# Reading turned activations and ready-made vector columns at the opening of a two-block transformer kernel

## The reference

```python
def rmsnorm(x, g):
    xf = x.astype(jnp.float32)
    y = xf * lax.rsqrt(jnp.mean(xf * xf, axis=-1, keepdims=True) + EPS)
    return (y * g.astype(jnp.float32)).astype(x.dtype)

h = rmsnorm(x, pre_mix_g[l])
proj = h @ w_in[l]

def ada_modulation(cond, w, b):
    m = jax.nn.silu(cond) @ w + b
    return jnp.split(m[..., None, :], N_MOD, axis=-1)
```

## Time and profile before

| | |
|---|---|
| Median of 3 runs | 2143.29 us (2139.48 to 2143.92) |
| Profiled execution | 2144.96 us, span 2143.3 us |
| PE busy | 2119.4 us, 99% |
| DVE busy | 1563.8 us, 73% |
| ACT busy | 1092.7 us, 51% |
| POOL busy | 128.7 us, 6% |
| DMA | 487.10 MB, mean 227 GB/s; 332 GB/s in the first of 40 slices |
| Granted TensorE clock | 0.999 |

### The profile page before, as it was taken

One profiled execution on the slowest core, in us unless ns is written; L12 is line 12 of the kernel. 1 busy time (PEld: TensorE's weight loads), 2 busy tenths in 40 slices (PEclk: granted clock), 3 DMA queues, 4 the chain that ended last, 5 costly groups with the idle time before them and its releaser, 6 DMA issues.

```text
span 2143.3 us, 33221 instructions
## 1 busy us (share of the span) xinstructions
PE 2119.4 (99%) x10603; PEld 1764.0 (82%) x10603; DVE 1563.8 (73%) x1943; ACT 1092.7 (51%) x1499; POOL 128.7 (6%) x231
## 2 busy tenths in 40 slices
PE   8999999999999999999999999999999999999998
PEld 7888888888888888888878867888888888888886
DVE  7997889888998888768777654567556656655766
ACT  6545755655444554345587465454434434443444
POOL 3110000100000100100000000010000000000000
PEclk9999999999999999999999999999999999999999
DMA  9887177888888888877756542667667766766763
GB/s 332 293 272 243 40 281 239 279 292 275 280 285 288 276 289 272 293 252 243 238 180 199 184 130 80 196 203 245 202 197 235 217 196 221 231 188 216 221 182 108
DMA packets 279985, 487.10 MB, mean 227 GB/s; under 512 B 26252, under 2 KB 118740, under 8 KB 278560
## 3 DMA queue, kind: packets, MB, share of 16 engines
q1 hardware_dynamic: 249472, 371.42, 53.5%
q0 software_dynamic: 30192, 113.72, 16.5%
q10 hardware_dynamic: 176, 0.08, 0.0%
HBM read 483.00 MB, written 2.11 MB: 226 GB/s over the span
## 4 chain that ended last, share of the span: by engine, by line
PE 95%; ACT 2%; DVE 2%; DMA 1%; issue 1%; POOL 0%; ACTq 0%; DVEq 0%; POOLq 0%
PE G L2020 20%; PE G L2022 20%; PE G L2021 20%; PE G L2035 6%; PE T L2035 6%; PE G L2037 3%; PE T L2037 3%; PE T L2022 3%; PE T L2020 3%; PE T L2021 3%; PE T L2234 1%; PE T L2318 1%; PE T L2468 1%; ACT w_hi L602 1%; PE T L2074 1%; PE G L2450 1%
## 5 line engine op out<-in xcount | busy, mean ns | idle before, releaser
L1144 DVE TENSOR_TENSOR w_lo<-raw,w_hi 128x1024 fp32r<-128x1024 f32 (+1 forms) x704 | 851.8, 1217 | 470.1 <-ACT w_hi L602 466.8
L602 ACT ACTIVATE w_hi<-raw 128x1024 fp32r<-128x1024 f32 (+1 forms) x704 | 741.4, 1055 | 822.9 <-PE G L2022 532.8
L2020 PE MATMUL G<-w_hi,h_both 128*128 128x512 f32 (+1 forms) x1144 | 447.1, 391 | 2.0 <-DVE h_both L1236 1.7
L2022 PE MATMUL G<-w_hi,h_both 128*128 128x512 f32 (+1 forms) x1144 | 442.7, 387 | 0.0
L2021 PE MATMUL G<-w_lo,h_both 128*128 128x512 f32 (+1 forms) x1144 | 442.3, 387 | 0.0
L2020 PE MATMUL G<-w_hi,a_hi 128*128 128x512 f32 x880 | 345.9, 393 | 1.9 <-DVE w_lo L1144 1.2
L2022 PE MATMUL G<-w_hi,a_lo 128*128 128x512 f32 x880 | 342.7, 389 | 0.0
L2021 PE MATMUL G<-w_lo,a_hi 128*128 128x512 f32 x880 | 342.5, 389 | 0.0
L2020 PEld LDWEIGHTS G<-w_hi,h_both 128*128 128x128 f32 x1144 | 215.1, 188 | 45.5 <-issue 3.7
L2022 PEld LDWEIGHTS G<-w_hi,h_both 128*128 128x128 f32 x1144 | 214.9, 188 | 44.1
L2021 PEld LDWEIGHTS G<-w_lo,h_both 128*128 128x128 f32 x1144 | 215.2, 188 | 41.9
(11 more groups left out here) (320 smaller groups left out, 2117.9 us busy)
## 6 DMA issues: line engine op xcount, KB each, us to landing
ada_w<-in_w_ada POOLq DMA_DIRECT2D x192, 512.0 KB, 5.0
raw<-in_w_up SPq DMA_DIRECT2D x352, 256.0 KB, 4.4
raw<-in_w_mlp_up SPq DMA_DIRECT2D x256, 256.0 KB, 2.9
raw<-in_w_mlp_down SPq DMA_DIRECT2D x256, 256.0 KB, 3.2
raw<-in_w_in SPq DMA_DIRECT2D x224, 256.0 KB, 3.8
raw<-in_w_down SPq DMA_DIRECT2D x176, 256.0 KB, 4.5
raw<-in_w_out SPq DMA_DIRECT2D x128, 256.0 KB, 3.5
raw<-in_w_in SPq DMA_DIRECT2D x16, 136.0 KB, 3.4
```

The costliest lines, as they stand in the source:

```text
L602: act.activation(w_hi[:, s % 4, :, 0:width], raw[:, s % 8, :, 0:width], ACT.Copy).then_inc(hi_ready, 1)
L1144: dve.tensor_tensor(w_lo[:, s % 4, :, 0:width], raw[:, s % 8, :, 0:width], w_hi[:, s % 4, :, 0:width].bitcast(F32), ALU.subtract).then_inc ...
L2020: pe.matmul(out, ah, wh, start=f, stop=False)
L2022: mm = pe.matmul(out, al, wh, start=False, stop=l)
```

## The change

The program gets two more arrays, laid out on the host: x transposed (`x_turned`, 2048 x 256) and all small vectors as columns (`columns`, 128 x 568: 120 for gains and conditions, 352 for the convolution, 96 for the bias). Their single vectors are no longer passed. `xt` takes the turned x in eight pieces of two tiles, and ACT and DVE make the high and low part of h from it and `gains` directly. Token-major x is still loaded, after the first four loads of weights (eight steps) and all turned pieces; each square waits for its piece. All transposes of x and of vectors are gone, and with them DVE's four copies; `keep_busy` goes from 2 and 6 to 16 at the start. The waits on the new arrivals are `xt_in[q]` in `first_high`, `vec_in` (one DMA) ahead of ACT's and DVE's lists, `vec2_in` ahead of the first `in1_evac` and in `first_vectors`. POOL's wait for `x_in[3]` and DVE's order of `w_lo` and tiles are unchanged.

```diff
@@ sync
+        def xt_piece(q):
+            sp.dma_start(xt[:, 2 * q:2 * q + 2, :], tiles(a["x_turned"])[:, 2 * q:2 * q + 2, :]).then_inc(xt_in[q], 16)
...
-        x_piece(0)
-        x_piece(1)
-        for k in range(4):
+        xt_piece(0)
+        for k, pieces in enumerate(((1, 2), (3, 4), (5, 6, 7), ())):
             load(l0 + k, w_in1[:, LOADK * k:LOADK * k + LOADK, 0:N])
-            if k < 2:
-                x_piece(k + 2)
+            for q in pieces:
+                xt_piece(q)
+        for g in range(4):
+            x_piece(g)
@@ gpsimd
-        for v in rows:
-            n = v.shape[0] // P
-            pool.dma_start(stage[r0:r0 + n, 0, :], v.rearrange("(t p) -> t p", p=P)).then_inc(vec_in, 16)
...
-        for k in range(3):
-            pool.dma_start(stage[0:CTS, 1 + k, :], a["conv_w"][0, k].rearrange("(t p) -> t p", p=P)).then_inc(vec2_in, 16)
-        pool.dma_start(stage[0:CTS, 4, :], a["conv_b"][0].rearrange("(t p) -> t p", p=P)).then_inc(vec2_in, 16)
-        pool.dma_start(stage[0:96, 5, :], a["b_ada_2"][0].rearrange("(t p) -> t p", p=P)).then_inc(vec2_in, 16)
+        pool.dma_start(convw[:].rearrange("p a b -> p (a b)"), a["columns"][:, 120:120 + 4 * CTS]).then_inc(vec2_in, 16)
+        pool.dma_start(bada[:], a["columns"][:, 120 + 4 * CTS:]).then_inc(vec2_in, 16)
         pool.memset(ada_acc[:], 0.0).then_inc(ada_zero, 1)
         pool.wait_ge(x_in[3], 16)
@@ scalar
+        act.dma_start(gains[:], a["columns"][:, 0:120]).then_inc(vec_in, 16)
         act.dma_start(consts[:], a["table"][:, C_ID:C_TRI]).then_inc(table_in, 16)
-        act.dma_start(stage[0:KT, 6, :], a["pre_mix_g"][0].rearrange("(t p) -> t p", p=P)).then_inc(pre_in, 16)
...
         def first_high(q):
-            high("in1", q, premix, h_hi)
+            act.wait_ge(xt_in[q], 16)
+            for k in (2 * q, 2 * q + 1):
+                ins = act.activation(h_hi[:, k, :], xt[:, k, :], ACT.Copy, scale=gains[:, PRE_MIX + k:PRE_MIX + k + 1])
+            ins.then_inc(prep_hi, 1)
 
         def x_squares(g):
+            act.wait_ge(x_in[g], 16)
             squares(g, lambda b: x[:, b, g * N:g * N + N])
@@ vector
         def first_low(q):
-            low("in1", q, premix, h_hi, h_lo)
+            dve.wait_ge(prep_hi, PREP["in1"] + q + 1)
+            for k in (2 * q, 2 * q + 1):
+                ins = dve.scalar_tensor_tensor(out=h_lo[:, k, :], in0=xt[:, k, :], scalar=gains[:, PRE_MIX + k:PRE_MIX + k + 1],
+                                               in1=h_hi[:, k, :].bitcast(F32), op0=ALU.mult, op1=ALU.subtract)
+            ins.then_inc(h_ready, 1)
@@ tensor
         pe.wait_ge(table_in, 16)
-        keep_busy(2)
-        turns("in1", x, 0, 1)
...
-        turns("in1", x, 1, 4)
...
-        pe.transpose(G[:, 3, P:P + 120], stage[0:120, 0, :], ident[0:120, 0:120]).then_inc(vec_turned, 1)
-        keep_busy(6)
+        keep_busy(16)
...
-        steps(s0, 0, 2, 0, H, r)
-        turns("in1", x, 4, 6)
-        steps(s0, 2, 3, 0, H, r)
-        turns("in1", x, 6, 8)
-        steps(s0, 3, 8, 0, H, r)
+        steps(s0, 0, 8, 0, H, r)
...
-        in1_steps(1, 0, 3)
-        pe.wait_ge(vec2_in, 16 * 5)
-        for k in range(4):
-            pe.transpose(T[:, 1, k * CTS:(k + 1) * CTS], stage[0:CTS, 1 + k, :], ident[0:CTS, 0:CTS])
-        pe.transpose(T[:, 2, 0:96], stage[0:96, 5, :], ident[0:96, 0:96]).then_inc(vec2_turned, 1)
-        in1_steps(1, 3, 8)
+        in1_steps(1, 0, 8)
```

More of the change, by code:

```diff
@@ L198, in build @@
     junk = place("junk", [P, N], "tmp", 8 * KB_)
-    stage = place("stage", [P, 7, P], "y", 4 * KB_)
+    xt = place("xt", [P, KT, TOK], "act", 16 * KB_)
     consts = small("consts", [P, P + 8])
@@ L205, in build @@
     gains = small("gains", [P, 120])
-    premix = small("premix", [P, KT])
     convw = small("convw", [P, 4, CTS])
@@ L245, in build @@
     x_in = [sem(f"x_in{g}") for g in range(4)]
-    pre_in, pre_turned, pre_ready, pre_hi = sem("pre_in"), sem("pre_turned"), sem("pre_ready"), sem("pre_hi")
+    xt_in = [sem(f"xt_in{q}") for q in range(8)]
     table_in, vec_in, vec2_in, misc_in = sem("table_in"), sem("vec_in"), sem("vec2_in"), sem("misc_in")
@@ L253, in build @@
         sem("base_ready"), sem("tap1"), sem("gelu_done"), sem("conv_used"), sem("a_first"), sem("a_ready"))
-    vec_turned, vec2_turned, cols_ready, cols2_ready, silu_e = (
-        sem("vec_turned"), sem("vec2_turned"), sem("cols_ready"), sem("cols2_ready"), sem("silu_e"))
+    silu_e = sem("silu_e")
     ada_full = [sem("ada_full0"), sem("ada_full1")]
@@ L299, in build @@
     PREP = {"in1": 0, "out1": 8, "up1": 16, "ctx": 24, "in2": 32, "out2": 40, "up2": 48}
-    TURNED = {"in1": 0, "out1": 8, "up1": 16, "ctx": 24, "in2": 32, "out2": 36, "up2": 44}
+    TURNED = {"out1": 0, "up1": 8, "ctx": 16, "in2": 24, "out2": 28, "up2": 36}
     NORMED = {"out1": 0, "ctx": 8, "in2": 16, "up2": 24}
@@ L440, in _ @@
     def _(pool):
-        rows = [a["c_2"][0], a["c_ctx_2"], a["pre_mix_g"][0], a["grp_swa_g"][0], a["grp_fox_g"][0], a["pre_ffn_g"][0],
-                a["norm_attn_w_2"][0], a["norm_mlp_w_2"][0], a["pool_scale_2"][0]]
-        r0 = 0
-        for v in rows:
-            n = v.shape[0] // P
-            pool.dma_start(stage[r0:r0 + n, 0, :], v.rearrange("(t p) -> t p", p=P)).then_inc(vec_in, 16)
-            r0 += n
-        assert r0 == 120
         pool.dma_start(sink1[:], a["sinks"].broadcast_to([P, HEADS])).then_inc(misc_in, 16)
@@ L625, in evac @@
                 act.activation(dst(b), G[:, 2 * parity + b, 0:width], func, scale=scale).then_inc(bank_evac, 1)
-        act.wait_ge(table_in, 16)
-        act.activation(unused[:], ident[:, 0:1], ACT.Exp)
-        act.wait_ge(pre_ready, 1)
+        act.wait_ge(vec_in, 16)
+        act.activation(unused[:], gains[:, 0:1], ACT.Exp)
         s0 = 2 * FIRST_LOAD["in1"]
         def first_high(q):
-            high("in1", q, premix, h_hi)
+            act.wait_ge(xt_in[q], 16)
+            for k in (2 * q, 2 * q + 1):
+                ins = act.activation(h_hi[:, k, :], xt[:, k, :], ACT.Copy, scale=gains[:, PRE_MIX + k:PRE_MIX + k + 1])
+            ins.then_inc(prep_hi, 1)
         def x_squares(g):
+            act.wait_ge(x_in[g], 16)
             squares(g, lambda b: x[:, b, g * N:g * N + N])
@@ L645, in _ @@
         first_high(3)
-        act.wait_ge(cols_ready, 1)
         act.activation(silu[:].rearrange("p a b -> p (a b)"), gains[:, 0:32], ACT.Exp, scale=-1.0).then_inc(silu_e, 1)
@@ L687, in turned1 @@
             ins.then_inc(qk_act, 1)
+        act.wait_ge(vec2_in, 32)
+        act.wait_ge(table_in, 16)
         act.wait_ge(rstd_ready, STAT["in1"] + 1)
@@ L1247, in _ @@
         dve.memset(ones_col[:], 1.0)
-        dve.wait_ge(pre_turned, 1)
-        dve.tensor_copy(premix[:], G[:, 3, 0:KT]).then_inc(pre_ready, 1)
-        dve.wait_ge(pre_ready, 1)
+        dve.wait_ge(vec_in, 16)
         s0 = 2 * FIRST_LOAD["in1"]
         def first_low(q):
-            low("in1", q, premix, h_hi, h_lo)
+            dve.wait_ge(prep_hi, PREP["in1"] + q + 1)
[3 more added lines that the diff above has]
+            ins.then_inc(h_ready, 1)
         def silu_columns():
@@ L1280, in _ @@
         lo(s0 + 1)
-        dve.wait_ge(vec_turned, 1)
-        dve.tensor_copy(gains[:], G[:, 3, P:P + 120]).then_inc(cols_ready, 1)
-        dve.wait_ge(cols_ready, 1)
         first_low(2)
@@ L1298, in first_vectors @@
         def first_vectors():
[L1300 to L1303, removed]
+            dve.wait_ge(vec2_in, 32)
             dve.wait_ge(misc_in, 48)
+            dve.wait_ge(table_in, 16)
             for n, sink in enumerate((sink1, sink2)):
@@ L2067, in turn @@
                 pe.wait_ge(x_new, X_NEW[name] + q + 1)
-            if name == "in1" and q % 2 == 0:
-                pe.wait_ge(x_in[q // 2], 16)
             if q >= 4:
@@ L2168, in turn1_qk @@
             pe.wait_ge(bank_evac, 2 * g + 2)
-            if g == 0:
-                pe.wait_ge(cols2_ready, 1)
             if g == 2:
@@ L2563, in build @@
     ctx.close()
[L2566 to L2569, removed]
+NAMES = ["x", "w_in", "b_forget", "sinks", "w_out", "post_mix_g", "w_up", "w_down", "post_ffn_g", "ctx_2",
+         "w_ada_2", "b_ada_2", "w_in_2", "attn_sink_2", "pool_w_2", "w_out_2", "w_mlp_up_2", "w_mlp_down_2", "final_norm_w_2"]
+VECTORS = ["c_2", "c_ctx_2", "pre_mix_g", "grp_swa_g", "grp_fox_g", "pre_ffn_g", "norm_attn_w_2", "norm_mlp_w_2", "pool_scale_2",
+           "conv_w", "conv_b", "b_ada_2"]
 def kernel(**inputs):
@@ L2578 @@
     arrays, aps = {}, {}
-    for name, value in [(n, inputs[n]) for n in NAMES] + [("table", table), ("pool_table", pool_table)]:
+    vectors = [np.asarray(inputs[n]).reshape(-1, P) for n in VECTORS]
+    columns = np.concatenate(vectors, axis=0).T
+    x_turned = np.asarray(inputs["x"])[0].T
+    for name, value in [(n, inputs[n]) for n in NAMES] + [("table", table), ("pool_table", pool_table),
```

(1 more changed line is left out.)

5 lines of the change are left out of this document (removed).

## The result

| | before | after |
|---|---|---|
| Median | 2142.34 us (10 runs, 2139.48 to 2143.92) | 2147.26 us (10 runs, 2145.20 to 2149.49) |
| Ratio | | 1.0027, 95% interval 1.0019 to 1.0035 |
| Profiled execution | 2144.96 us | 2145.2 us, span 2143.5 us |

The account below looks back on a forecast made before the run. PE, busy 2119.4 of 2143.3 us, was taken as the bound; the 4.6 us won lie wholly inside the wait caused by DVE's late first tile, leaving 2.5 us slower: 2145.8 us from the median 2143.29, range 2139.0 to 2149.3.

Parts of the forecast that it names:

- What comes off PE: Opening and first projection on PE: transposes gone and step 0 earlier, 2.5 + 1.75 + 0.38 = 4.6 us offered.
- I take 9.8 for step 0: First projection's first matmul on PE: starts at 9.8, 2.5 us earlier, after fillers and step 0's weights.
- x's fourth piece: Last token-major piece on SyncE's queue, which lets POOL start the tiles: at 28.7 instead of 17.99.
- ACT's wait before step 2: ACT waits for the fourth turned piece ahead of w_hi 2: step 2 ready at 17.6, PE wants it at 16.2.
- Tile: First w_ada tile on POOL's queue: lands 8.1 us after its issue, as before.
- X = 37.3: Landing of the first w_ada tile: at 37.3, 6 us after DVE took it before.
- DVE's order behind X: DVE's in-order list from first tile through w_lo 9 and 10, root, second tile and w_lo 11: done at X + 10.5.
- Step 9 is ready at X + 3.7: First projection's step 9: ready at 41.0, PE wants it at 36.6, a wait of 4.4 us.
- w_lo 14 ends at X + 19.0: DVE's w_lo of step 14: ends at 56.3, so step 14 is 2.5 us later than 53.8 before.
- DVE isn't held: Rival at DVE's first tile: it comes by 33, step 14 at 50.2, 3.6 us faster, 2139.7; chance 0.18.
- PE falls to half clock: Rival behind PE's wait: steps 9 and 10 at 0.43 us a matmul, 5.7 us slower, 2149.0; chance 0.11.
- my signs: DVE idle 3 to 7 us, PE 3 to 5; fourth piece past 27; first matmul 9 to 10.5; step 14 55 to 58.

Follow-up runs that it names:

- e4: Changed kernel with POOL's fill of ada_acc moved ahead of its five DMAs; 2146.86 us, ratio 1.0023 to the kernel before.
- e5: Changed kernel with POOL's two DMAs of vector columns moved behind the first two w_ada tiles; one run, 2147.91 us.
- e6: Changed kernel with POOL's three broadcast DMAs (sinks, forget bias) moved behind the first two w_ada tiles; one run, 2144.92 us.
- e2: Changed kernel with 20 filler matmuls of 512 columns on PE behind step 8; 2146.44 us, ratio 1.0019 to the kernel before.
- e7: Changed kernel reordered: x between loads of steps 8 to 15, tiles at eighth turned piece, table, broadcasts, columns and squares later, w_hi 2 earlier; 2140.88 us, ratio 0.9998.
- e9: Kernel of e7 with squares, root and first evacuation later and the table behind the sixth tile; 2137.13 us, ratio 0.9979 to the kernel before.
- e11: Kernel before with vectors as columns and three broadcasts behind the first two w_ada tiles, x still transposed on PE; 2139.51 us, ratio 0.9988.
- e12: Kernel before with only the three broadcasts moved behind the first two w_ada tiles; 2141.47 us against 2141.41, ratio 1.0001.
- e10: Changed kernel with 42 filler transposes of the identity on PE behind step 8; one run, 2146.21 us.
- e3: Kernel before with POOL starting table and tiles when w_lo of step 7 is made, not at x's fourth piece; 2145.41 us, ratio 1.0018.
- e1: Changed kernel with POOL starting table and tiles at the eighth turned piece instead of x's fourth piece; 2145.17 us, ratio 1.0015 to the kernel before.

## Why the prediction was right, and where it was off

**The direction and the mechanism were right.** I forecast 2.5 us slower, 2145.8; measured were 4.9, 2147.26, in the range. The time is nearer than the difference by luck: the median that I counted from lay 0.95 us above that of the ten runs. I called it most likely indistinguishable; the ratio is 1.0027, past the line that I had drawn at 0.2%, though the interval's lower end, 1.0019, touches it.

**What comes off PE.** "I take 9.8 for step 0": 10.68. The table was early (4.55 instead of 5.3 to 6.5); the weights, which I put at 6.3, were used at 8.26. The failed step is the rate: I took 394 GB/s, and it was 152 from 5 to 8. That the small loads would move into that stretch stood in the change, and I costed POOL's shorter list at nothing. It is what e4, e5 and e6 found. My reason, that nobody waits, looked at POOL's fill and left out its DMAs, and every byte up to x's fourth piece is waited for.

**ACT's wait before step 2**: foreseen, and there: ACT waited 1.56 us at the fourth turned piece. But it cost PE almost nothing, since PE came late itself behind twelve slow matmuls: step 2 started at 18.96, forecast 17.6, and step 9 was wanted at 38.1, forecast 36.6. Of the 3.2 us by which PE was to be ahead there, 1.5 were left, and the wait took these too.

**x's fourth piece** at 28.7: 29.73, 1.0 late, for the same reason (27.75 in e6). **Tile** 8.1 us: 8.9. So **X = 37.3**: 39.15.

**DVE's order behind X.** "Step 9 is ready at X + 3.7": 42.99 is X + 3.8, and the wait was 4.7 us, forecast 4.4. "w_lo 14 ends at X + 19.0": 55.72 + 1.23 is X + 17.8, 1.2 less. ACT had done the square root's table load while DVE was held, so DVE waited 0.27 us for the root instead of 1.15, which is 0.9 of it; the rest lies in w_lo 9 and 10, which now followed each other without a wait.

**The two rivals.** *DVE isn't held* fell: 6.01 us of idle. *PE falls to half clock* I gave 0.11, and it came, in part: nine slow matmuls, where I had priced 24. They take 46.71 - 42.99 = 3.7 us instead of 9 x 0.227 = 2.0, and since PE was then no longer held by w_lo 11 or 14, 1.4 of these 1.7 us stayed (58.31 against 56.95, under e2). The count isn't fixed: 12 and 14 slow matmuls followed the like wait in e5 and e6 (3.91 and 4.59 us), and there step 14 started 2.2 and 2.6 us behind the end of its w_lo. I had set the point from which it decides at 3 us of slow matmuls, with 1.4 us hidden before step 11; with the root cheaper there was nothing to hide it in.

**The sum as measured** at step 14: 2.5 forecast, + 1.9 for X, - 1.2 for the root, + 1.4 for the clock = 4.6. The first matmul of step 14 before and after, in PE's timeline:

```profile
53.68 0.39 PE L2020 MATMUL G<-w_hi,h_both 128*128 128x512 f32 x1
...
58.31 0.39 PE L2013 MATMUL G<-w_hi,h_both 128*128 128x512 f32 x1
```

That is 4.6 too, and so says the mark. Of the extra 1.9 for X, 1.0 is x's fourth piece and 0.8 the tile's landing. In e6, without the slow stretch, the piece came at 27.75 and the tile at 37.02, 2.1 us earlier than in the changed kernel and near the 37.3 of the forecast. Of my signs, the waits of DVE and PE and the fourth piece past 27 came as named; the first matmul (10.68, said 9 to 10.5) and step 14 (58.31, said 55 to 58) lay just outside.

## What to carry to other kernels

A transfer that "comes later" has to be followed through everything that waits for it, not only its reader: here the fourth piece of x was the starting signal of another stream, and an engine that works in order had that stream's first tile ahead of the weights. When a load's consumer is taken away from the critical path, move the load, its consumers in each in-order list, and the signals hung on it together: the same bytes in another order are 5 us faster instead of 5 slower. And each of the four unfilled waits of PE of 3.9 to 4.7 us here cost more than its length, so fill such a wait or split it.

## What the runs showed that I had not expected

- A broadcast DMA can cost far more than its bytes. In the first 13 us three of 8 KB took a full DMA stretch to between 125 and 193 GB/s for 2 to 3 us in each place where they stood (5 to 8, 6 to 8, 8 to 11, 11 to 13). Behind the first two tiles, in five kernels (e6, e7, e9, e11, e12), the stretch of 3 or 4 us around their landing still moved 343 GB/s or more. The difference is not explained.
- PE after a wait of 4.7 us ran nine matmuls at 0.43 us (granted clock 0.57 over 4 us); after 1.1 to 1.3 us of waiting, as before step 2 in e2 and e10, and after 2.9 in e7, it ran at full pace. Length alone doesn't decide: in e4 a wait of 2.4 us before step 9 was followed by five fast matmuls and then by eight slow ones. Forty-two transposes of the identity in the wait prevented it as well as twenty matmuls did.
- The first 512 KB tile on POOL's queue took 8.1 us before and 8.9 after, and only 6.4 in e3, issued 0.6 us later than in after; the least of the early tiles took 3.8.
- In the opening the slow stretch of PE is not reproducible: 12 matmuls in the changed kernel, 10 in e2 and none in e1, e6, e11 or e12, at starts between 9.7 and 11.9. That is up to 2.4 us of scatter in any mark there.
